# Quads with V as TensorE's weights in the attention of layer 0, and rows of the first stage asked for on GpSimd's queue

## What is computed

```python
a = modulate(rmsnorm(h, g_mix), shift, scale)       # shift, scale: silu(c) @ w_ada + b_ada
cq, ckv, kr, qs, ks, vs = split_last(a @ w_in, EVEN_SPLITS)
q = (rmsnorm(cq, g_q) @ w_uq)                        # 8 heads of 96
kv = (rmsnorm(ckv, g_kv) @ w_ukv)                    # 8 heads: 64 of k, 64 of v
...
def full_attention(q, k, v):                         # kind 0: latent tokens see all 768 keys
    s = jnp.einsum('bqhd,bkhd->bhqk', q, k).astype(jnp.float32) * (q.shape[-1] ** -0.5)
    p = jax.nn.softmax(s, axis=-1).astype(v.dtype)
    return jnp.einsum('bhqk,bkhd->bqhd', p, v)

def softmax_with_sink(s, sink):                      # kind 1: a window of 128 and the context
    m = jnp.maximum(s.max(axis=-1, keepdims=True), sink)
    e = jnp.exp(s - m)
    return e / (e.sum(axis=-1, keepdims=True) + jnp.exp(sink - m))
...
y = jnp.concatenate([o_mla, o_swa], axis=-1) @ w_out
```

## Time and profile before

| what | us |
| --- | --- |
| median of 3 runs (lowest, highest) | 2706.31 (2701.83, 2713.14) |
| the profiled execution | 2705.75 |
| its span | 2703.9 |
| PE busy in the span | 2386.5 (88%) |
| first stage | 0 to 281 |
| attention of layer 0 | 281 to 551 |
| stage after it | 551 to 670 |

### The profile page before, as it was taken

One profiled execution on the slowest core, in us unless ns is written; L12 is line 12 of the kernel. 1 busy time (PEld: TensorE's weight loads), 2 busy tenths in 40 slices (PEclk: granted clock), 3 DMA queues, 4 the chain that ended last, 5 costly groups with the idle time before them and its releaser, 6 DMA issues. The chain is left out here.

```text
span 2703.9 us, 34801 instructions
## 1 busy us (share of the span) xinstructions
PE 2386.5 (88%) x13838; PEld 1317.8 (49%) x13838; DVE 824.6 (30%) x1655; ACT 647.6 (24%) x1389; POOL 270.3 (10%) x253
## 2 busy tenths in 40 slices
PE   7899899988899999999994679998779989888874
PEld 3445577776544333333331678886645333333321
DVE  2232345544720000000001855555462000000005
ACT  1111333432012211112112344444311111111111
POOL 1000000021111111111111000000211111111100
PEclk9999899998899999999997799999879999999997
DMA  8465300022359999999994711100337999999967
GB/s 320 172 218 194 119 1 1 1 83 86 147 223 347 388 378 376 403 380 379 373 364 161 274 67 42 36 30 1 137 140 273 412 411 409 419 415 387 418 283 295
DMA packets 122207, 646.59 MB, mean 239 GB/s; under 512 B 18648, under 2 KB 29912, under 8 KB 60352
## 3 DMA queue, kind: packets, MB, share of 16 engines
q1 hardware_dynamic: 93088, 558.31, 52.9%
q0 software_dynamic: 28672, 85.02, 8.0%
q10 hardware_dynamic: 288, 1.05, 0.1%
HBM read 604.38 MB, written 57.75 MB: 245 GB/s over the span
## 5 line engine op out<-in xcount | busy, mean ns | idle before, releaser
L1475 PE MATMUL E_psG<-E_gu,E_xT 128*32 128x512 f32 (+2 forms) x2576 | 533.3, 621 | 42.9 <-DMA E_gu<-in_we_up_dram 27.0
L1769 DVE TENSOR_TENSOR E_hh<-E_sil,E_psG 128x256 f32<-128x256 f32 x96 | 40.4, 421 | 1091.9 <-ACT E_sil L1608 1091.9
L1475 PE MATMUL E_psG<-o,E_xT 128*32 128x512 f32 (+2 forms) x912 | 273.4, 608 | 18.3 <-DMA E_gu<-in_we_up_dram 18.3
L1475 PEld LDWEIGHTS E_psG<-E_gu,E_xT 128*32 128x32 f32 (+2 forms) x2576 | 159.2, 123 | 264.4 <-issue 258.2
L1489 PE MATMUL E_psY<-E_dn,E_hT 128*32 128x512 f32 (+1 forms) x1288 | 261.8, 596 | 1.5 <-ACT E_hT L1611 1.5
L1608 ACT ACTIVATE E_sil<-E_psG 128x256 f32<-128x256 f32 x96 | 36.9, 384 | 667.5 <-PE E_psG L1475 667.5
L1350 POOL DMA_INDIRECT y_d<-E_yb,E_sca x94 | 94.1, 1001 | 993.1 <-ACT E_yb L1614 993.1
L1614 ACT ACTIVATE E_yb<-E_psY,E_wgt 128x1024 f32<-128x1024 f32 x96 | 107.0, 1114 | 289.4 <-PE E_psY L1489 289.4
L1475 PE MATMUL E_psG<-raw,E_xT 128*32 128x512 f32 (+2 forms) x464 | 148.4, 594 | 1.2 <-DVE E_xT L1766 1.2
L1475 PE MATMUL E_psG<-fT,E_xT 128*32 128x512 f32 (+2 forms) x496 | 148.4, 594 | 0.5 <-ACT E_xT L1605 0.5
L1489 PE MATMUL E_psY<-o,E_hT 128*32 128x512 f32 (+2 forms) x456 | 134.4, 596 | 0.0
(11 more groups left out here) (382 smaller groups left out, 3740.2 us busy)
## 6 DMA issues: line engine op xcount, KB each, us to landing
E_gu<-in_we_gate_dram SPq DMA_DIRECT2D x78, 1024.0 KB, 4.7
E_gu<-in_we_up_dram SPq DMA_DIRECT2D x78, 1024.0 KB, 6.8
E_dn<-in_we_down_dram SPq DMA_DIRECT2D x78, 1024.0 KB, 6.8
h<-in_w_ada_dram SPq DMA_DIRECT2D x40, 1024.0 KB, 4.8
o<-in_we_gate_dram SPq DMA_DIRECT2D x26, 1024.0 KB
o<-in_we_up_dram SPq DMA_DIRECT2D x26, 1024.0 KB
o<-in_we_down_dram SPq DMA_DIRECT2D x26, 1024.0 KB
I_ring<-y_d SPq DMA_DIRECT2D x24, 1024.0 KB, 7.0
```

The lines of the kernel that those rows point to most:

```text
L1475: ins = nc.tensor.matmul(psG[c:c + n, 0].rearrange("p (v f) -> p v f", v=2), xT[:, k, c:c + n], slots[s][0][:, :, k], start=(k == 0), stop ...
```

## The change

1. `rows(2)` to `rows(5)` are asked for on POOL's queue, with the same waits there and semaphores of their own (`s_hp`). SP's waits for `s_an` are gone.
2. In the attention the sinks are asked for ahead of `x` and `ctx`.
3. Units are grouped in quads: in kind 0 two token tiles by two heads, in kind 1 four heads of one tile. Both kinds of the latent tiles come first, then the context's. Two units of a quad with the same V share one product: V (64 columns) is PE's weights, and 256 columns of turned probabilities move. The two V of a quad write to partitions 0 to 63 and 64 to 127 of `psO`, so the output comes turned: [head x 64, token]. The products of a quad are spread over four iterations (`values(Q, part)`), 3 to 6 iterations behind its last scores.
4. Since tokens are now columns, the reciprocal of the sums must be turned too. DVE (`sums`) takes the reciprocal of each sum spread over 64 elements, [128, 256] a quad; PE turns it in two transposes into `psO`; ACT copies it to `bsum`; DVE (`divide`) multiplies and writes to `o` in its new layout `oT`.
5. The stage after takes `o` turned as it is: no turns of `o` on PE in layer 0; ACT and DVE read from SBUF. SP's wait ahead of the shared expert's weights is for `s_ol` instead of the last turn.

The diff, cut to its core, with 12 columns of indentation taken away:

```diff
@@ -292,10 +293,7 @@
...
             def rows(t):
-                if t >= 2:
-                    sp.wait_ge(s_an, t - 1)
-                src = a["x"][0, t * P:(t + 1) * P] if t < NL else a["ctx"][0, (t - NL) * P:(t - NL + 1) * P]
-                sp.dma_start(h[:, t % 2], src).then_inc(s_hin[t % 2], 16)
+                sp.dma_start(h[:, t % 2], a["x"][0, t * P:(t + 1) * P]).then_inc(s_hin[t % 2], 16)
@@ -334,14 +332,8 @@
...
-            rows(2)
-            rows(3)
             for i in range(KD, STEPS):
                 q, k = divmod(i, KD)
-                if i == 10:
-                    rows(4)
-                if i == 17:
-                    rows(5)
@@ -367,13 +359,22 @@
...
+            for t in range(2, NT):
+                pool.wait_ge(s_an, t - 1)
+                src = a["x"][0, t * P:(t + 1) * P] if t < NL else a["ctx"][0, (t - NL) * P:(t - NL + 1) * P]
+                pool.dma_start(h[:, t % 2], src).then_inc(s_hp[t % 2], 16)
+            for b in range(2):
+                pool.wait_ge(s_hp[b], 16 * (NT // 2 - 1))
...
-                act.wait_ge(s_hin[t % 2], 16 * (t // 2 + 1))
+                if t < 2:
+                    act.wait_ge(s_hin[t], 16)
+                else:
+                    act.wait_ge(s_hp[t % 2], 16 * (t // 2))
@@ -703,8 +704,16 @@
...
-units = [(t, kind, hd) for t in range(NT) for kind in range(2) for hd in range(8)]
-N = len(units)
+quads = [(0, t, j) for j in range(4) for t in (0, 2)] + [(1, t, j) for t in range(NL) for j in (0, 2)]
+quads += [(0, NL, j) for j in range(4)] + [(1, t, j) for t in range(NL, NT) for j in (0, 2)]
+NQ = len(quads)
+N = 4 * NQ
+def unit(i):
+    kind, t, j = quads[i // 4]
+    x, s = divmod(i % 4, 2)
+    return (t + x, kind, 2 * j + s) if kind == 0 else (t, kind, 2 * j + 2 * x + s)
@@ -712,20 +721,37 @@
...
+oT = o[:].rearrange("p t d -> p (t d)").rearrange("p (c n) -> p c n", c=KD)
+def out_of(Q):
+    kind, t, j = quads[Q]
+    if kind == 0:
+        return oT[:, j, t * P:(t + 2) * P].rearrange("p (x n) -> p x n", x=2)
+    return oT[:, 4 + j:6 + j, t * P:(t + 1) * P]
...
-    pT = sb(ctx, "C_pT", [P, 2, NT, P])
+    pT = sb(ctx, "C_pT", [P, 2, 2, NT, 2 * P])
...
+    rsum = sb(ctx, "C_rsum", [P, 2, 4, MV])
+    bsum = sb(ctx, "C_bsum", [P, 2, P])
...
-    psO = ps(ctx, "C_psO", [P, 2, 512])
+    psO = ps(ctx, "C_psO", [P, 2, 2, 2, P])
@@ -735,9 +761,9 @@
...
+            sp.dma_start(sink[:], a["wa_sink"][0:1, :].to_broadcast([P, 8])).then_inc(s_sink, 16)
             sp.dma_start(h[:, 0:NL], a["x"][0].rearrange("(t p) d -> p t d", p=P)).then_inc(s_h, 16)
             sp.dma_start(h[:, NL:NT], a["ctx"][0].rearrange("(t p) d -> p t d", p=P)).then_inc(s_h, 16)
-            sp.dma_start(sink[:], a["wa_sink"][0:1, :].to_broadcast([P, 8])).then_inc(s_sink, 16)
@@ -764,116 +790,136 @@
...
-            def values(i):
-                t, kind, hd = units[i]
-                pe.wait_ge(s_evd, i + 1)
-                pe.wait_ge(s_eva, i + 1)
-                g = i // 8
-                if i % 8 == 0 and g >= 2:
-                    pe.wait_ge(s_o, g - 1)
+            def values(Q, part):
+                kind, t, j = quads[Q]
                 ks, _ = keys(t, kind)
-                for n, k in enumerate(ks):
-                    v = vM[:, k, hd * MV:(hd + 1) * MV] if kind == 0 else vS[:, k, hd // 4 * SD:hd // 4 * SD + SD]
-                    ins = nc.tensor.matmul(psO[:, g % 2, hd * 64:(hd + 1) * 64], pT[:, i % 2, n], v, start=(n == 0), stop=(n == len(ks) - 1))
-                ins.then_inc(s_pv, 1)
-            for i in range(N + 3):
+                if part == 0:
+                    pe.wait_ge(s_evd, 4 * Q + 4)
+                    pe.wait_ge(s_eva, 4 * Q + 4)
+                    if Q >= 2:
+                        pe.wait_ge(s_o, Q - 1)
+                c = [len(ks) * n // 4 for n in range(5)]
+                for n in range(c[part], c[part + 1]):
+                    for s in range(2):
+                        hd = 2 * j + s
+                        v = vM[:, ks[n], hd * MV:(hd + 1) * MV] if kind == 0 else vS[:, ks[n], hd // 4 * SD:hd // 4 * SD + SD]
+                        ins = nc.tensor.matmul(psO[64 * s:64 * s + 64, Q % 2, 0].rearrange("p x n -> p (x n)"), v, pT[:, Q % 2, s, n],
+                                               start=(n == 0), stop=(n == len(ks) - 1))
+                if part == 3:
+                    ins.then_inc(s_pv, 1)
+                    pe.wait_ge(s_rs, Q + 1)
+                    for x in range(2):
+                        ins = nc.tensor.transpose(psO[:, Q % 2, 1, x], rsum[:, Q % 2, 2 * x:2 * x + 2].rearrange("p s d -> p (s d)"), ident)
+                    ins.then_inc(s_b, 1)
+            for i in range(N + 6):
                 if i < N:
                     scores(i)
                 if 2 <= i < N + 2:
                     turn(i - 2)
-                if i >= 3:
-                    values(i - 3)
+                if i >= 6:
+                    values((i - 6) // 4, (i - 6) % 4)
...
+                if Q >= 2 and i % 4 == 0:
+                    dve.wait_ge(s_pv, Q - 1)
...
-                nc.vector.tensor_copy(pT[:, i % 2, 0:f], psP[:, 0, 0:f]).then_inc(s_evd, 1)
-            def divide(g):
-                t, kind = g // 2, g % 2
-                sl = ssum[:, g]
-                if kind == 1:
-                    dve.wait_ge(s_se, t + 1)
-                    link(nc.vector.tensor_tensor(sl, sl, sdif[:, t % 2], ALU.add))
+                V.tensor_copy(pT[:, Q % 2, s, 0:f, x * P:(x + 1) * P], psP[:, 0, 0:f]).then_inc(s_evd, 1)
+            def sums(Q):
+                sl = ssum[:, Q]
+                if quads[Q][0] == 1:
+                    w = windows.index(Q)
+                    dve.wait_ge(s_se, w + 1)
+                    link(V.tensor_tensor(sl, sl, sdif[:, w % 2], ALU.add))
                 else:
-                    dve.wait_ge(s_e, 8 * g + 8)
-                link(nc.vector.reciprocal(sl, sl))
-                dve.wait_ge(s_pv, 8 * g + 8)
-                nc.vector.tensor_tensor(o[:, t, kind * 512:(kind + 1) * 512].rearrange("p (h d) -> p h d", d=64),
-                                        psO[:, g % 2].rearrange("p (h d) -> p h d", d=64), bcl(sl, 64), ALU.mult).then_inc(s_o, 1)
-            for i in range(N + 4):
+                    dve.wait_ge(s_e, 4 * Q + 4)
+                if Q >= 2:
+                    dve.wait_ge(s_b, Q - 1)
+                link(V.reciprocal(rsum[:, Q % 2], bcl(sl, MV)), s_rs)
+            def divide(Q):
+                dve.wait_ge(s_bs, Q + 1)
+                dve.wait_ge(s_pv, Q + 1)
+                V.tensor_tensor(out_of(Q), psO[:, Q % 2, 0], bsum[:], ALU.mult).then_inc(s_o, 1)
+            for i in range(N + 8):
                 if i < N:
                     maximum(i)
+                if i % 4 == 0 and 0 <= i // 4 - 1 < NQ and quads[i // 4 - 1][0] == 1:
+                    Q, w = i // 4 - 1, windows.index(i // 4 - 1)
+                    hd = 2 * quads[Q][2]
+                    if w >= 2:
+                        dve.wait_ge(s_se, w - 1)
+                    link(V.tensor_tensor(sdif[:, w % 2], sink[:, hd:hd + 4], nmax[:, Q], ALU.add), s_sd)
                 if 2 <= i < N + 2:
                     evac(i - 2)
-                if i % 8 == 1 and i > 8 and (i // 8 - 1) % 2 == 1:
-                    g = i // 8 - 1
-                    if g // 2 >= 2:
-                        dve.wait_ge(s_se, g // 2 - 1)
-                    link(nc.vector.tensor_tensor(sdif[:, g // 2 % 2], sink[:], nmax[:, g], ALU.add), s_sd)
-                if i >= 11 and (i - 11) % 8 == 0:
-                    divide((i - 11) // 8)
+                if i % 4 == 2 and 0 <= (i - 6) // 4 < NQ:
+                    sums((i - 6) // 4)
+                if i % 4 == 3 and 0 <= (i - 11) // 4 < NQ:
+                    divide((i - 11) // 4)
...
-                    nc.scalar.activation(pT[:, j % 2, f:n], psP[:, 1, 0:n - f], ACT.Copy).then_inc(s_eva, 1)
-                if i % 8 == 1 and i > 8 and (i // 8 - 1) % 2 == 1:
-                    g = i // 8 - 1
-                    act.wait_ge(s_sd, g // 2 + 1)
-                    nc.scalar.activation(sdif[:, g // 2 % 2], sdif[:, g // 2 % 2], ACT.Exp).then_inc(s_se, 1)
+                    if Q >= 2 and j % 4 == 0:
+                        act.wait_ge(s_pv, Q - 1)
+                    nc.scalar.activation(pT[:, Q % 2, s, f:n, x * P:(x + 1) * P], psP[:, 1, 0:n - f], ACT.Copy).then_inc(s_eva, 1)
...
+                if i % 4 == 2 and 0 <= (i - 10) // 4 < NQ:
+                    Q = (i - 10) // 4
+                    act.wait_ge(s_b, Q + 1)
+                    if Q >= 1:
+                        act.wait_ge(s_o, Q)
+                    nc.scalar.activation(bsum[:], psO[:, Q % 2, 1], ACT.Copy).then_inc(s_bs, 1)
@@ -888,6 +934,8 @@
...
+turned = gain_in is None
+oT = o[:].rearrange("p t d -> p (t d)").rearrange("p (c n) -> p c n", c=KD)
@@ -922,14 +970,15 @@
...
-    uses = [("O", 0)]
+    uses = [] if turned else [("O", 0)]
     for t in range(nt + 1):
```

(51 more changed lines are left out.)

32 lines of the change are left out of this document (16 added, 16 removed).

## The result

The changed kernel takes 2684.11 us (median of 4 runs, 2680.81 to 2688.82), the kernel before 2705.01 in the same comparison: a ratio of 0.9922, with a 95% interval of 0.9906 to 0.9937. The forecast was 2680 in 2658 to 2697. The profiled execution took 2680.81 us, so in the two profiles the gain is 24.9 us, in the medians 20.9.

What follows compares the result with a forecast made beforehand. The prediction took PE as the bound in layer 0's attention, busy 244 of 250 us. Its terms, 12.5 + 9.9 - 1.2 + 4.3 = 25.5 us, came off 2705.75 to give 2680 us, range 2658 to 2697.

Steps and rivals of the forecast that it cites:

- A: First stage: rows 2 to 5 on POOL's queue end the stalls for `w_ada` pieces, 12.5 us won.
- D: Stage after the attention: without turns of `o` on PE, 4.3 us won.
- B: Start of the attention: sinks asked for first let VectorE begin earlier, 9.9 us won.
- C: Attention in quads: gains in six-key units and windows against losses in context and at the end, 1.2 us lost in sum.
- Rival 4: First stage only exchanges its stall, so rows on POOL's queue give 0: 2692 us, chance 0.08.
- C, six-key quads: Attention's six-key units: a quad takes 12.1 us against 13.2, 8.8 us won over 32 units.
- C, latent quads in sum: Attention's six-key units and windows together: 8.8 and 6.2 us won.
- C, context: Attention's context units: 1.9 us each against 1.45, 14.4 us lost, and 1.8 more at the stage's end.
- rival 3: Context units: the clock falls, half of the units at half clock, 16 us, 2696 us; chance 0.10.
- Rival 1: Attention's value products: the halves don't run two at a time, 42 us more, 2722 us; chance 0.03.
- Rival 2: Reciprocal in `sums` is cheap, 0.4 us, so its delays go: 20 us less, 2660 us; chance 0.14.
- The fifth: Rival on `sums`: by the documentation page's rule each reciprocal takes 2.1 us, total 2688 us; chance 0.10.

Runs made afterwards that it cites:

- short form: Changed kernel with the reciprocal taken of a quad's 4 sums, then spread by a copy, instead of of 256 elements: 2665.38 us, on another chip 2668.81 us.

## Why the prediction was right, and where not

The total was right, and so was the order of the parts; several terms held errors that cancel, and one rival came true in part. That the sum came within 1 us in the profiles is luck in that sense: A and D were 3.7 us too low together, B and C 4.3 too high. By medians, 20.9 us, the forecast was 4.6 too high.

- **A, rows on POOL's queue: 12.5 forecast, 14.3 in the two profiles, 13.4 and 13.8 by taking it away and by giving it alone.** Right, the stall goes and nothing takes its place. The 0.9 to 1.8 us over are of the size by which the start of the attention scatters between profiles of the same first stage (267.57 to 269.82 us for first scores). Rival 4 is excluded.
- **B, the sink first: 9.9 forecast, 8.8 at `nsink`.** The 8.5 for the earlier load was right. The term of 1.4 us for the fill and the clock was wrong: the second scores come as long behind the first maximum as before (2.03 and 2.04 us), and the half clock lasts 8.9 us behind it instead of 7.7. PE's idle time there went from 9.10 to 2.92 us, not to 1.
- **C, six-key quads: 12.1 forecast, 12.04 measured, for the wrong reason.** I had 11.5 us of PE and 0.57 of delay behind the reciprocal. The short form shows PE alone at 11.96: its turns take 0.76 instead of 0.66 now that they stand beside halves (four a quad), and the values 3.2 instead of 3.08, together the 0.5 that I was short. The reciprocal costs 0.08 us a quad, and 0.13 in the windows, where I had 0.5 to 0.66: it is hidden, since PE, busy 36.00 of 36.00 us with either form, has other work meanwhile.
- **C, latent quads in sum: 15.0 won by forecast, 15.6 measured** (before 101.0 and 104.2 us for six keys and windows, after 94.2 and 95.4). Two errors cancel in it: the six keys won 6.8 instead of 8.8, since eight such units took 24.9 to 25.8 us before and not the 26.3 of 3.29 each, and the windows won 8.8 instead of 6.2.
- **C, context: 16.2 lost by forecast (14.4 and the end's 1.8), 20.0 measured** (51.0 us before, 71.1 after). By the short form's 57.0 us, 6 of them are lost without the wide reciprocal, 6 more with it at the full clock, and 8 by the clock. At the full clock the quads take 6.6 and 7.2 us, where I had 1.9 a unit, 7.6: this term was too large by some 4 us. What came on top is rival 3, which I held for one in ten: from 499 the clock is at its half, and the last quads take 8.4, 9.8 and 10.1 instead of 7.2, the end 5.8 instead of 4.5 (4.5 is my estimate: 3.7 to 4.5 us were seen with the short form, so it may be more, and the clock's share less). That is 1.2 + 2.6 + 2.9 + 1.3 = 8 us, half of the 16 that I gave the rival, since it took in the last 10 or 11 of the 32 units and not 16. The step that failed is "against: the gap of 1.45 at 28.25 left a step of 1.07": one gap says nothing of a gap in each second unit for 38 us.
- **D, no turns of `o`: 4.3 forecast, 6.2 measured.** 2.0 us at the start, as worked out. Each further tile gained 16.08 - 15.26 = 0.82 (three of them, 2.5, forecast 2.7 in all), and the last part, from the start of the shared product to that of the last turns of `f`, went from 8.52 to 6.92 us: before, the granted clock was at its half for the first 3.2 us of it. I had no term for that. The 0.4 charged for the clock at the stage's start did not show: it was at its half for 6.8 us there before and 6.9 after.
- **Rival 1** (halves not together, 2722) is excluded by 0.22 us a pair, and its price was tested: made to run one by one they give 2717, 5 us under the rival's 2722.
- **Rival 2** (a cheap reciprocal, 2660) was wrong for this kernel, since the reciprocal takes 1747 ns; my estimate of 1.81 us, from 353 ns for 32 elements and 6.5 ns for each further one, was 4% over. As a rewritten kernel it came to 2665 and 2669. Its price of 20 us for the delays is about what was measured, 18.7, but not from where I had it: of the 20, 9 were to come from latent quads, and 1.7 did (8 x 0.08 and 1.1).
- **The fifth** (2.1 us a reciprocal) did not come true: 1747 ns for 256 elements, the mean of 24 instructions, are 6.8 ns each with all that is fixed. The page "VectorE: DVE Perf Modes" of the Trainium skill ("First, the fixed hardware budget") gives the reciprocal's divide a repeat count of 8; my estimate from it, with the 0.96 GHz of its Specifications, was 8.3 ns an element, and the trace does not agree.

By profiles the sum was 25.5 and came to 24.9: +1.8 for A, -4.3 for B and C, +1.9 for D, and nothing in the end for the stages behind, where 2.3 us were won at the start of the first experts and lost by the last ones. By medians it is 4 us less: 3.3 since the profiled execution is the fastest of its four, and 0.7 since that of the kernel before lies above its median.

## What to carry to other kernels

Ask of each part of a large edit what it brings alone: here a reordered load of 4 KB and four loads moved to another queue brought all of the gain, and the rewritten attention none, until its one costly operation, a reciprocal over a broadcast view, was cut to the four elements that differ. What an operation on an engine off the path costs depends on what the path has to do meanwhile: the same 1.75 us were hidden in long units and laid bare in short ones. And where a change thins out PE's work in a stretch, read the granted clock there before and after: the time may go with it, as it did here, with 8 us in the last 33 of the stage.

## What the runs showed of the hardware

- The reciprocal grows by 6.2 ns an element between 32 (353 ns) and 256 (1747 ns), and 128 elements took 0.94 to 0.95 us; a copy with the same broadcast source takes 294 ns on VectorE and 396 on GpSimd.
- Pairs of 128 by 64 products of 256 columns on the two halves of PE's columns take 0.22 us a pair at the full clock, 0.14 a group on top; in sequence on one half each takes 0.213.
- The issue of the same 4 KB load took SyncE 0.33 us as the first of the stage and 1.83 behind two loads of 1 and 2 MB; its data came 3.5 and some 11 us after the issue.
- The clock fell 38 us into the context units in the changed kernel and with the rows back on SyncE's queue, 30 with the sinks last and with both undone, 29 with the reciprocal in halves, 20 with it short in the latent quads only, 48 with one half at a time, 57 with the scores twice, and only in or behind the last quad (53 us in or later) with the short form in the context quads. In the 10 us ahead of the fall PE was busy 7.0 to 7.9 us in the first six, 8.5 with one half at a time and 8.7 with the scores twice; with the short form it was busy 8.3 of 10 and the clock held. No wait of PE in the 30 us ahead of any of these falls was longer than 1.3 us. What decides is open; no run varied one property alone, and each kernel was profiled once.
